# Outputs of seven head pairs stored in two parts and added by GpSimd's accumulating transfers in a two-block transformer kernel

## What is computed

```python
# second block, cut
qa, ka, va, fa, qc, kc, vc, gates = jnp.split(h @ w_in[l], SPLITS, axis=-1)
o_a = from_heads(forgetting_attention(heads(qa), heads(ka), heads(va), log_f))   # 8 fox heads
o_b = from_heads(chunk_band_attention(heads(qc), heads(kc), heads(vc), rel_bias[l]))  # 8 chunk heads
g_a, g_b = jnp.split(jax.nn.sigmoid(gates), 2, axis=-1)
merged = g_a * (o_a @ w_branch_a[l]) + g_b * (o_b @ w_branch_b[l])
x = x + merged @ w_out[l]
# in each head: p = softmax(q k^T * scale + bias);  o = p v
```

## Time and profile before

| | |
|---|---|
| median of 3 runs | 1795.58 us |
| the profiled execution, its own time | 1795.7 us |
| its span, first to last instruction | 1793.9 us |
| TensorE busy (page, part 1) | 1778.1 us, 99% |
| VectorE busy | 1367.7 us, 76% |
| ScalarE busy | 870.9 us, 49% |
| GpSimd busy | 506.7 us, 28% |
| granted TensorE clock, mean of the execution | 0.998 of full speed |
| mean transfer rate | 128 GB/s |

### The profile page before, as it was taken

The page is one execution under the profiler, slowest core; times in us unless marked ns, Lnnn a source line. Parts: engine busy times, 40 slices in busy tenths (PEclk is TensorE's granted clock), DMA queues, the critical chain, the costliest instruction groups (busy, mean ns, idle before and its releaser), DMA issues.

```text
span 1793.9 us, 25231 instructions
## 1 busy us (share of the span) xinstructions
PE 1778.1 (99%) x8831; PEld 1494.6 (83%) x8831; DVE 1367.7 (76%) x2587; ACT 870.9 (49%) x1690; POOL 506.7 (28%) x449
## 2 busy tenths in 40 slices
PE   9999999999999999999999999999999999999998
PEld 7888888877888888888888878888888878888887
DVE  7698674888544798888889797697667678777777
ACT  6697234545333576666666434352223234344334
POOL 0110010013222011123323152026566654324223
PEclk9999999999999999999999999999999999999999
DMA  6101413333333322222226427434444477546343
GB/s 217 44 25 37 147 36 106 130 138 111 112 118 106 103 77 77 73 83 80 70 70 206 142 89 233 147 103 141 159 162 155 159 276 271 178 155 229 100 129 130
DMA packets 84413, 229.71 MB, mean 128 GB/s; under 512 B 8960, under 2 KB 16448, under 8 KB 81216
## 3 DMA queue, kind: packets, MB, share of 16 engines
q1 hardware_dynamic: 83728, 227.67, 38.2%
q10 hardware_dynamic: 560, 0.43, 0.1%
HBM read 163.55 MB, written 55.08 MB: 122 GB/s over the span
## 4 chain that ended last, share of the span: by engine, by line
PE 87%; DVE 7%; ACT 3%; issue 2%; DMA 1%; POOL 0%; POOLq 0%; SPq 0%; DVEq 0%; ACTq 0%
PE D L1084 53%; PE S L1084 14%; PE T L1084 6%; PE PV L1451 4%; PE T L1417 3%; PE S L1389 2%; PE S L1390 2%; PE D L1125 1%; DVE Wl L2179 1%; ACT SPs L2504 1%; DVE xe L2140 1%; PE S L1125 1%; DVE T L2272 1%; DMA T<-f_scratch 0%; DVE SPs L1662 0%
## 5 line engine op out<-in xcount | busy, mean ns | idle before, releaser
L2777 ACT CAST Wh<-Wr 128x1024 fp32r<-128x1024 f32 (+2 forms) x198 | 156.8, 792 | 281.1 <-PE D L1084 175.0
L1084 PE MATMUL D<-Hh,Wh 128*128 128x512 f32 x1000 | 263.7, 394 | 1.3 <-DVE xe L2140 1.3
L1084 PE MATMUL D<-Hl,Wh 128*128 128x512 f32 x1000 | 261.9, 392 | 0.0
L1084 PE MATMUL D<-Hh,Wl 128*128 128x512 f32 x1000 | 261.5, 392 | 0.0
L1084 PEld LDWEIGHTS D<-Hh,Wl 128*128 128x128 f32 x1000 | 184.4, 188 | 35.7
L2179 DVE TENSOR_TENSOR Wl<-Wr,Wh 128x512 fp32r<-128x512 f32 (+2 forms) x185 | 183.7, 993 | 39.7 <-ACT Wh L2777 38.9
L1084 PEld LDWEIGHTS D<-Hh,Wh 128*128 128x128 f32 x1000 | 183.3, 188 | 36.7 <-DVE xe L2140 1.7
L1084 PEld LDWEIGHTS D<-Hl,Wh 128*128 128x128 f32 x1000 | 184.2, 188 | 35.1
L2777 ACT CAST Wh<-Sx 128x512 fp32r<-128x512 f32 (+1 forms) x120 | 70.5, 592 | 146.8 <-PE D L1084 77.2
L2179 DVE TENSOR_TENSOR Wl<-Sx,Wh 128x512 fp32r<-128x512 f32 (+1 forms) x120 | 105.9, 890 | 22.3 <-ACT Wh L2777 21.7
L2516 ACT ACTIVATE SP<-SP,sm 128x640 f32<-128x640 f32 (+7 forms) x128 | 94.5, 738 | 56.1 <-DVE sm L1695 55.5
(11 more groups left out here) (405 smaller groups left out, 3806.0 us busy)
## 6 DMA issues: line engine op xcount, KB each, us to landing
Wr<-w SPq DMA_DIRECT2D x62, 512.0 KB, 3.5
f_scratch<-xe SPq DMA_DIRECT2D x28, 768.0 KB, 4.8
Wr<-wdn SPq DMA_DIRECT2D x36, 512.0 KB, 4.3
Wr<-wo SPq DMA_DIRECT2D x32, 512.0 KB, 3.5
Wr<-wup SPq DMA_DIRECT2D x27, 512.0 KB, 4.1
T<-f_scratch SPq DMA_DIRECT2D x11, 1024.0 KB, 7.1
Hl<-f_scratch SPq DMA_DIRECT2D x10, 1024.0 KB, 6.3
K<-K SPq DMA_DIRECT2D x32, 256.0 KB, 3.2
```

The costliest lines, as they stand in the source:

```text
L1084: m = e.matmul(into, (low if n == 2 else high)(k), (operand_low if n == 1 else operand_high)(k), start=begin and (n, k) == todo[0], stop=( ...
L2777: e.copy(high, src).then_inc(*raised("act_weights", x))
```

## The change

For ADDED = range(7), the pairs of index 0 to 6 in the order PAIRS (56 of the 64 units), the output of a unit isn't added on the chip. ScalarE copies all 128 rows of PV into osb in one instruction of 128x256, and this frees PV; VectorE's add is left out. SyncE waits for ScalarE and stores both halves, 128 KB, into a scratch with one more dimension (part 0 and part 1). When both last outputs of a pair have landed, GpSimd issues a transfer of 512 KB from part 1 into part 0 that accumulates (accum_op add); it also waits for its transfer of the pair before. The loads of the outputs wait for that addition. They are now two transfers, for the even and the odd head of the pair, 64 rows each, also for the last pair, whose outputs are otherwise made as before. The planner gets a new stream on GpSimd, dma_added, at rank 1.

```diff
-    oad = nc.dram_tensor("oa_scratch", (4, 128, 1024), F32, kind="Internal").ap()
-    obd = nc.dram_tensor("ob_scratch", (4, 128, 1024), F32, kind="Internal").ap()
+    oad = nc.dram_tensor("oa_scratch", (4, 2, 2, 64, 1024), F32, kind="Internal").ap()
+    obd = nc.dram_tensor("ob_scratch", (4, 2, 2, 64, 1024), F32, kind="Internal").ap()
...
+        ADDED = range(7)
...
+        def output_ready(w, pr):
+            if pr in ADDED:
+                w.wait_ge(*at("dma_added", pr))
+            else:
+                for i in both:
+                    w.wait_ge(*at("dma_o%d" % i, (2 * pr + 1, 2 + i)))
...
                     x = ("p2", hd, j)
+                    if hd // 2 in ADDED:
+                        continue
                     w.wait_ge(*at("act_o", *x))
                     also(("clear",) + x, "dve_o", *x)
                     e.tensor_tensor(osb[0:64, i % 2, :], PV[0:64, 0:256], osb[0:64, i % 2, :], ALU.add).then_inc(
...
-                    e.copy(osb[0:64, i % 2, :], PV[64:128, 0:256]).then_inc(*raised("act_o", *x))
+                    if hd // 2 in ADDED:
+                        also(("clear",) + x, "act_o", *x)
+                        e.copy(osb[:, i % 2, :], PV[:, 0:256]).then_inc(*raised("act_o", *x))
+                    else:
+                        e.copy(osb[0:64, i % 2, :], PV[64:128, 0:256]).then_inc(*raised("act_o", *x))
...
+            def added_outputs():
+                for pr in ADDED:
+                    for i in both:
+                        w.wait_ge(*at("dma_o%d" % i, (2 * pr + 1, 2 + i)))
+                    od = (oad if fox(2 * pr) else obd)[PAIRS[pr] % 4]
+                    if pr:
+                        w.wait_ge(*at("dma_added", pr - 1))
+                    e.dma_start(od[:, 0], od[:, 1], accum_op=ALU.add, max_dma_last_dim=4096).then_inc(*landed("dma_added", pr))
+                    yield load(1024)
...
-                        src = obd[x[1]]
+                        to, src = to[64:128, :], obd[x[1], 1, 0]
+                        e.dma_start(raw_at(r)[0:64, :], obd[x[1], 0, 0]).then_inc(*landed("dma_w%d" % r, x, "first"))
...
-                    w.wait_ge(*at("dve_o", "p2", hd, j))
-                    e.dma_start((oad if fox(hd) else obd)[h // 2, hh * 64:hh * 64 + 64, j * 256:j * 256 + 256],
-                                osb[0:64, i, :]).then_inc(*landed("dma_o%d" % i, (hd, j)))
-                    yield load(64)
+                    to = (oad if fox(hd) else obd)[h // 2, hh, :, :, j * 256:j * 256 + 256]
+                    if hd // 2 in ADDED:
+                        w.wait_ge(*at("act_o", "p2", hd, j))
+                        e.dma_start(to.rearrange("a p c -> (a p) c"), osb[:, i, :]).then_inc(*landed("dma_o%d" % i, (hd, j)))
+                    else:
+                        w.wait_ge(*at("dve_o", "p2", hd, j))
+                        e.dma_start(to[0], osb[0:64, i, :]).then_inc(*landed("dma_o%d" % i, (hd, j)))
+                    yield load(64 * (1 + (hd // 2 in ADDED)))
...
-                for i in both:
-                    w.wait_ge(*at("dma_o%d" % i, (2 * PAIRS.index(k) + 1, 2 + i)))
+                output_ready(w, PAIRS.index(k))
                 also(("ld_oa", k), "dma_or%d" % k)
-                e.dma_start(o_raw[k % 2][:, k // 2, :], oad[k]).then_inc(*landed("dma_or%d" % k))
+                e.dma_start(o_raw[k % 2][0:64, k // 2, :], oad[k, 0, 0]).then_inc(*landed("dma_or%d" % k, "first"))
+                e.dma_start(o_raw[k % 2][64:128, k // 2, :], oad[k, 1, 0]).then_inc(*landed("dma_or%d" % k))
```

More of the change, by code:

```diff
@@ L3021, in squares @@
                     yield pool2(H // 2)
-            return {"pool_norm": (0, 0, norms()), "pool_weights": (2, 0, lows()), "pool_bias": (1, 0, bias()), "pool_mixed": (0, 0, mixed()),
+            def added_outputs():
[7 more added lines that the diff above has]
+                    yield load(1024)
+            return {"dma_added": (1, 0, added_outputs()), "pool_norm": (0, 0, norms()), "pool_weights": (2, 0, lows()), "pool_bias": (1, 0, bias()), "pool_mixed": (0, 0, mixed()),
                     "pool_sums": (1, 0, differences()), "pool_wsums": (2, 0, weight_sums()),
@@ L3037, in weights_into @@
                     if x[0] == "ob":
-                        for i in both:
-                            w.wait_ge(*at("dma_o%d" % i, (2 * PAIRS.index(4 + x[1]) + 1, 2 + i)))
+                        output_ready(w, PAIRS.index(4 + x[1]))
                     kb, kind = 512, x[0]
```

## The result

The changed kernel took 1817.6 us (median of 4 runs, 1817.42 to 1817.73), against 1795.9 us for the kernel before in the same job: a ratio of 1.0118, 95% interval 1.0106 to 1.0131. Forecast were 1794.5 us, with a range that ended at 1801.0. The prediction was wrong: the change costs 22 us.

What follows compares the result with a forecast made beforehand. TensorE was taken to bound the kernel, busy 1778.1 of 1793.9 us. The terms -1.1 - 1.5 + 1.1 + 0.4 = -1.1 us took 1795.6 to 1794.5 us, with a range of 1789.5 to 1801.0.

Steps and rivals of the forecast that it cites:

- (5): The 512 KB additions: some 4 us spread, 23 us on two engines; covered by 56 us before their load, so nothing.
- Rival B: Burst behind the seventh pair, from 958.56 us: its addition delays an output store, ScalarE's copy waits; +6, 1801.6 us; chance 0.10.
- (6): Output loads cut in two: eight more SyncE issues of 0.33 us, near a reader only from 1009.42 us; nothing.
- (1): 56 of 64 VectorE adds (L1766) go, 23.0 us; TensorE gains 1.1 us of idle and 1.5 of hidden hold-ups.
- Rival A: Attention, 600 to 1015 us: hold-ups go with VectorE's load, issues cost nothing; 5.8 us faster, 1789.8; chance 0.24.
- (2): ScalarE's copy covers 128 rows, not 64, 373 against 370 ns: nothing; PV comes free 0.4 us or more earlier.
- (3): SyncE's 56 output stores of 128 KB land in about 2.2 us, covered by about 10 us except in the burst.
- (4): GpSimd's seven issues, 1.1 us each; four lie among bias rows, a quarter may reach TensorE: +1.1 us.
- Rival C: GpSimd's issues and VectorE's row normalising (L1724) block one another: 6.8 us slower, 1802.4; chance 0.08, shared with late bias rows.
- (7): Other transfers slowed beside the additions: ScalarE's wait of 1.54 us grows by a quarter, 0.4 us.
- (8): The planner orders every queue of the kernel anew: no readable sign, 2 us on either side.

Runs made afterwards that it cites:

- the mended layout: Changed kernel with scratch as [4, 2 parts, 128 rows, 1024]: 128-row additions, whole loads, stores in two issues; 1794.79 us with seven pairs, 1793.75 with six.

## Why the prediction was wrong, step by step

**(5) is the step that failed.** It bounded the addition well (23 us on 2 engines; alone it takes 23.9, in place 26 to 29), and named the rule for the engines. Then it asked a single question, who waits for the addition, found 56 us of cover, and concluded that the sum is the same by either bound. The question left out was who else is on these two engines. By an estimate each load, store and weight of the burst is, for an eighth of its bytes (2 of 16 engines), and a transfer lands with its slowest share. On two engines the seven additions cost 17.0 us more than as one for each head, and nearly all of it is the seventh (16.8 us by the run with six): the cover of 56 us was true and beside the point. The cost isn't of the burst alone either. With two-engine additions TensorE's idle time of 600 to 955 us is 1.43 to 3.20 us in four runs, with one addition for each head 0.56 and 0.87, and in the kernels that leave out the adds and have no addition, or the mended layout, 0.00. A slow transfer's readers are cheap to find in the trace; its neighbours are the ones that paid.

**Rival B had the place and a tenth of the chance, and its price was too low.** It even said that every transfer ends by its slowest engine. Two of its terms were off, and it left one reader out. The overlap: the prediction let the addition start at 953.2, so that 15 of its 23 us met the burst. But the last store of the pair was issued at 955.38 instead of 951.26, landed after 3.09 us instead of 2, the issue followed 0.7 us behind that landing, and the addition ran from 959.14 to 988.2, practically all of it beside the burst. The delay: 7.5 us more for the output store were assumed. It landed after 21.8 us instead of 10.3, so 11.5 more, and it was issued at 974.58 instead of 967.66, 6.9 us later, because SyncE itself was held: its issues of the four halved output loads ahead of it lasted 1.2, 3.4, 3.1 and 0.8 us, those of the two whole ones 1.05 together. Both make the 18.5 us by which the copy starts later (996.48 for 977.97). The reader: B looked at the copy and not at the cast that stands ahead of it in the same queue, whose load took 28.0 us instead of 9. The cast's transfer landed at 992.8, the copy's at 996.4, and with the cast out of the way the copy cost the same, so this last slip cost nothing in time. B's 8 us as the point from which it decides fits: additions of 5 to 9 us do no harm.

**(6) was mis-costed as well, for want of looking at all eight loads.** It counted issues (0.33 us each) and only the loads at 1009.42. The two at 961.85 go out in the fullest stretch of the attention, DMA share 0.99 in 960 to 970 us before, and had a reader that was waiting already (1.11 us at 970.51). There the cost isn't the issue but the engines' time: 5.4 us in all, measured alone on the kernel before, where "nothing" stood.

**(1) had the right size.** 2.6 us were taken, 2.0 (0.4 to 3.6) measured by the run without the adds. Of its account, one half is borne out ahead of 955 us: TensorE's idle time there, 1.36 us, is 0.00 in the two kernels that leave the adds out without any addition and in both of the mended layout, but a wait of 1.1 to 1.8 us just behind 955 takes most of it back. The other half, hold-ups hidden in the score matmuls, isn't seen: those of the earlier trace rows last 343 to 345 ns in these kernels. Where the rest of the gain lies stays open. In the stretch VectorE went from 359.00 to 340.19 us in the run without the adds, not to 336. Rival A falls with its 5.8 us, outside the 0.4 to 3.6.

**(2) holds.** 56 copies of 128x256 at 368 ns, against 370. The one wait of TensorE for the release of PV (1.54 us at 915.57) comes of a late store, that is of (5). **(3)** 2.2 us were taken for a store of 128 KB. It is 1.9 and 1.8 where no two-engine addition runs, 4.1 and 3.3 in the changed kernel: the estimate was good for the transfer alone, and the rest is (5) again, covered by the two buffers but for 3.5 us of ScalarE's waits, of which 1.5 us reached TensorE.

**(4) overpriced its effect.** An issue took 1.37 to 1.59 us, above my 1.1, yet VectorE's wait for the masks went down to 1.9 us and no wait of TensorE ahead of 955 us leads to an issue. Rival C, a lock between GpSimd's issue and VectorE, has no row: with the mended layout, seven issues of 0.8 to 1.4 us lie ahead of 955 us, and TensorE's idle time there is 0.00. **(7)** priced transfers "beside the additions" at 0.4 us, which was the right term of the sum for B's mechanism; 17.0 were measured in its place. **(8)** was not what moved the seventh pair's last store by 4 us. Every variant's order was made anew; that store is issued at 951.88 without additions and 951.36 in the mended layout (951.26 before), at 952.8 to 953.0 with one addition for each head, and at 955.4 to 956.1 with seven two-engine additions. That is (5) as well.

## What to carry over

When a transfer is added, work out from its view how many DMA engines it uses and for how long, then list the transfers that are in flight beside it, not only its own reader: each lands with its slowest share. Put the larger dimension outermost, and keep loads at 128 partitions where the engines are full. A cover counts only in front of a reader; an instruction at the head of an in-order queue, such as a cast for the next stage, turns any late transfer into a stall of everything behind it. And where a rival has the place right, price it with the whole overlap before it gets its chance.

## What the runs showed of the hardware

An accumulating transfer in DRAM costs 1.5 times a copy on all engines (5.21 against 3.44 us for 512 KB) and 1.9 times on two (23.86 against 12.77). An addition of [2, 64, 4 KB] took 1040 packets, 912 of them under 512 B, where one of 128 rows takes 144; GpSimd's issue of it lasted 1.4 us, of the other, alone, 0.85. In an idle time of TensorE of 17 us the granted clock went to its lower level; a wait of 3.26 us in the run with halved loads also left a stretch at 0.89. SyncE's issues of single gate loads, 0.5 to 0.7 us each before, last up to 5.0 us beside the seventh addition.
